# The first four modulation blocks as TensorE products with their weights resident, and the first two norms' sums and roots ahead of them, in a two-layer diffusion backbone

## What is computed

```python
def rms_norm(x):
    return x * lax.rsqrt(jnp.mean(x * x, axis=-1, keepdims=True) + EPS)
def modulate(h, shift, scale):
    return rms_norm(h) * (1 + scale) + shift
def adaln(cond, w_mod, b_mod):            # w_mod: 1024 x 6144 in each layer
    return jnp.split(jax.nn.silu(cond) @ w_mod + b_mod, 6, axis=-1)
...
sh1, sc1, g1, sh2, sc2, g2 = adaln(c, w_mod[i], b_mod[i])
csh1, csc1, ... = adaln(c_ctx, w_mod[i], b_mod[i])      # layer 0 only
out_l = mixer(modulate(h, sh1, sc1), modulate(hc, csh1, csc1), w_in, ...)
h = h + g1 * out_l
h = h + g2 * peer(modulate(h, sh2, sc2), ...)
```

## Time and profile before

| | us |
|---|---|
| median of 3 runs | 4152.5 (4149.3 to 4152.78) |
| the profiled execution, device time | 4150.12 |
| its span, first to last instruction | 4148.2 |
| TensorE busy | 3957.0 (95%) |
| VectorE busy | 2057.5 (50%) |
| ScalarE busy | 1258.6 (30%) |
| GpSimd busy | 825.1 (20%) |
| first projection matmul starts | 104.14 |

### The profile page before, as it was taken

The page is one execution under the profiler, slowest core; times in us unless marked ns, Lnnn a source line. Parts: engine busy times, 40 slices in busy tenths (PEclk is TensorE's granted clock), DMA queues, the critical chain, the costliest instruction groups (busy, mean ns, idle before and its releaser), DMA issues.

```text
span 4148.2 us, 46185 instructions
## 1 busy us (share of the span) xinstructions
PE 3957.0 (95%) x18280; PEld 3182.4 (77%) x18280; DVE 2057.5 (50%) x3962; ACT 1258.6 (30%) x1573; POOL 825.1 (20%) x364
## 2 busy tenths in 40 slices
PE   2998898999999999999999898999999999999998
PEld 2555566888888887888888577888888887888886
DVE  5655861594333433555555241891444415555555
ACT  1003443333444442111111333333444431111111
POOL 0000003444333330000000254444333330000000
PEclk9999899999999999999999899999999999999999
DMA  6561011144455555866665121344445446666663
GB/s 212 191 227 68 16 67 71 64 150 140 146 197 178 180 200 178 272 196 196 194 189 171 47 90 47 120 142 145 175 168 189 173 174 215 195 195 191 191 195 121
DMA packets 321578, 651.02 MB, mean 157 GB/s; under 512 B 18642, under 2 KB 151379, under 8 KB 300628
## 3 DMA queue, kind: packets, MB, share of 16 engines
q1 hardware_dynamic: 321364, 648.08, 47.5%
HBM read 511.69 MB, written 136.31 MB: 156 GB/s over the span
## 4 chain that ended last, share of the span: by engine, by line
PE 92%; DVE 5%; ACT 1%; issue 1%; DMA 1%; SPq 0%; DVEq 0%; ACTq 0%
PE ps L1077 34%; PE ps L1041 34%; PE ps L1053 6%; PE ps L888 5%; PE ps L963 4%; PE ps L1015 4%; PE ps L915 1%; PE ps L858 1%; PE ps L929 1%; PE ps L999 1%; DVE macc L1202 1%; PE ps L947 1%; DVE xm L1176 1%; PE ps L845 0%; DVE rinv L1172 0%
## 5 line engine op out<-in xcount | busy, mean ns | idle before, releaser
L1133 POOL TENSOR_TENSOR Ulo<-Uraw,Uhi 128x1024 fp32r<-128x1024 f32 x256 | 643.5, 2514 | 992.6 <-ACT Uhi L731 992.6
L1077 PE MATMUL ps<-Hhi,Vhi 128*128 128x512 f32 x2048 | 798.9, 390 | 20.8 <-DVE Hlo L1510 20.8
L1041 PE MATMUL ps<-xhi,Uhi 128*128 128x512 f32 x2048 | 808.8, 395 | 0.0
L1077 PE MATMUL ps<-Hlo,Vhi 128*128 128x512 f32 x2048 | 798.6, 390 | 0.0
L1077 PE MATMUL ps<-Hhi,Vlo 128*128 128x512 f32 x2048 | 798.4, 390 | 0.0
L1041 PE MATMUL ps<-xlo,Uhi 128*128 128x512 f32 x2048 | 797.5, 389 | 0.0
L1041 PE MATMUL ps<-xhi,Ulo 128*128 128x512 f32 x2048 | 797.4, 389 | 0.0
L1493 DVE TENSOR_TENSOR Vlo<-Vraw,Vhi 128x1024 fp32r<-128x1024 f32 x256 | 313.7, 1225 | 701.0 <-ACT Vhi L787 701.0
L787 ACT CAST Vhi<-Vraw 128x1024 fp32r<-128x1024 f32 x256 | 268.3, 1048 | 1123.0 <-PE ps L1077 1101.3
L1077 PEld LDWEIGHTS ps<-Hhi,Vhi 128*128 128x128 f32 x2048 | 385.6, 188 | 101.7 <-issue 21.6
L1077 PEld LDWEIGHTS ps<-Hhi,Vlo 128*128 128x128 f32 x2048 | 385.5, 188 | 80.4
(11 more groups left out here) (209 smaller groups left out, 4012.9 us busy)
## 6 DMA issues: line engine op xcount, KB each, us to landing
Uraw<-in_UT SPq DMA_DIRECT2D x128, 1024.0 KB, 5.3
Vraw<-in_V SPq DMA_DIRECT2D x256, 512.0 KB, 3.5
act_scratch<-act_st SPq DMA_DIRECT2D x256, 256.0 KB, 4.9
G_scratch<-G_st SPq DMA_DIRECT2D x32, 2048.0 KB, 8.1
act<-act_scratch SPq DMA_DIRECT2D x256, 256.0 KB, 3.5
Gin<-G_scratch SPq DMA_DIRECT2D x64, 1024.0 KB, 7.0
modw<-in_w_mod SPq DMA_DIRECT2D x48, 1024.0 KB, 5.1
ring<-in_query SPq DMA_DIRECT2D x8, 2048.0 KB, 7.9
```

Source lines behind the costliest of these rows:

```text
L1041: mm = nc.tensor.matmul(up_bank(m), w, x[:, k, :], start=(k == 0 and j == 0), stop=(k == KT - 1 and j == 2))
L1077: mm = nc.tensor.matmul(down_bank(d), w[m % 3][:, cols], x[m % 3][:, :], start=(m == 0 and j == 0), stop=(m == NT - 1 and j == 2))
L1133: nc.gpsimd.tensor_tensor(Ulo[slot][:, :, cols], Uraw[slot][:, :, cols], Uhi[(HP + m) % 3][:, :, :].bitcast(F32), ALU.subtract).then_inc(U ...
```

## The change

In words, by engine.

- **SP** loads the four first blocks whole (2 MB each) into one buffer of 64 KB per partition, `modall`, each with a semaphore of its own and with no wait, behind `ones`, `hT` and `ctxT`. The tables of the rotation go between block 0 and block 1, the first two chunks of projection weights before and after block 3, the other constants after them. The first half blocks of the later modulation now wait for 16 scaled tiles instead of 8.
- **ACT and PE** do the squares, their sums and the roots of both norms first, the latents ahead of the context now, with the squares in a buffer of their own (`sq0`).
- **PE** then forms the modulation itself (`modulation_by_rows`): for each block, for each of its 4 groups of 128 columns, 8 products over the feature tiles that add up in PSUM. 128 x 128 of `w_mod` is the stationary operand; `condS[:, k, :]`, two columns (both conditioning vectors), moves.
- **DVE** has no part in the sums of the first four blocks; `maccx` is gone. It forms EPS and reciprocals, then the modulation vectors, then scales.
- The first projection waits for its tiles one by one; `x_ready` 2*KT is asked for at the first job of chunk 1.

```diff
-        maccx = sb("maccx", 56, [P, 2, CW])
+        modall = sb("modall", 56, [P, 2 * D // CW, KT, CW])
+        rinvc = sb("rinvc", 124, [P, TC])
+        sq0 = sb("sq0", 198, [P, 2, T])
...
-        NORMS = [(ctxT, TC, xc, 0, sh1, sc1, 1), (hT, T, xm, 0, sh1, sc1, 0), (hT, T, xm, 0, sh2, sc2, 0),
+        NORMS = [(hT, T, xm, 0, sh1, sc1, 0), (ctxT, TC, xc, 0, sh1, sc1, 1), (hT, T, xm, 0, sh2, sc2, 0),
...
+            sp.dma_start(ones[:, :], a["ones"]).then_inc(consts_in, 16)
...
+            sp.dma_start(hT[:, :, :], a["xT"].rearrange("(k p) t -> p k t", p=P)).then_inc(h_in, 16)
+            sp.dma_start(ctxT[:, :, :], a["ctxT"].rearrange("(k p) t -> p k t", p=P)).then_inc(ctx_in, 16)
+            for c in range(NFIRST):
+                sp.dma_start(modall[:, c, :, :],
+                             a["w_mod"][0].rearrange("(k p) n -> p k n", p=P)[:, :, c * CW:(c + 1) * CW]
+                             ).then_inc(modall_in[c], 16)
...
+                if c >= 2:
+                    load_chunk(W_IN + c - 2)
...
-                    sp.wait_ge(x_scaled, KT)
+                elif mslot[m] == 2:
+
+                    sp.wait_ge(x_scaled, 2 * KT)
...
+            act_e.wait_ge(h_in, 16)
+            stats(0)
+            act_e.wait_ge(ctx_in, 16)
+            stats(1)
             act_e.wait_ge(mod_ready, 1)
-            norm(0)
-            norm(1)
+            shift(0)
+            shift(1)
...
+            def modulation_by_rows(i):
+
+                for j in range(4):
+                    col = (4 * i + j) * 2
+                    for k in range(KT):
+                        mm = nc.tensor.matmul(ps[:, 7, col:col + 2], modall[:, i, k, j * P:(j + 1) * P],
+                                              condS[:, k, :], start=(k == 0), stop=(k == KT - 1))
+                mm.then_inc(mod_mm, 1)
...
             norm(0)
 
-            pe.wait_ge(rinv_ready, 1)
+            pe.wait_ge(ms_ready, 1)
             norm(1)
-
-
+            for i in range(NFIRST):
+                pe.wait_ge(modall_in[i], 16)
+                modulation_by_rows(i)
...
+                if c == 1 and in_jobs[j - 1][4] == 0:
+                    pe.wait_ge(x_ready, 2 * KT)
                 for k in range(KT):
+                    if j == 0:
+                        pe.wait_ge(x_ready, k + 1)
...
+            dve.wait_ge(consts_in, 48)
+            stats(0)
+            stats(1)
+            modulation(0, 0, g1, 2)
+            dve.sem_inc(mod_ready, 1)
+            scaled(0)
+            scaled(1)
```

More of the change, by code:

```diff
@@ L270, in backbone @@
         consts_in = sem("consts_in")
-        x_in = sem("x_in")
+        h_in = sem("h_in")
+        ctx_in = sem("ctx_in")
+        tab_in = sem("tab_in")
+        modall_in = [sem(f"modall_in{c}") for c in range(2 * D // CW)]
         w_in = [sem(f"w_in{n}") for n in range(RING + 1)]
@@ L364, in backbone @@
         NH1 = 2 * NFIRST
-        mslot = [m % 2 if m < NH1 else m % 3 for m in range(2 * NCH)]
-        mbefore = [max([w for w in range(m) if mslot[w] == mslot[m]], default=None) for m in range(2 * NCH)]
-        mlanded = [16 * (1 + sum(mslot[w] == mslot[m] for w in range(m))) for m in range(2 * NCH)]
+        mslot = [m % 3 for m in range(2 * NCH)]
+        mbefore = [m - 3 if m - 3 >= NH1 else None for m in range(2 * NCH)]
+        mlanded = [16 * (1 + sum(mslot[w] == mslot[m] for w in range(NH1, m))) for m in range(2 * NCH)]
         MOD_AT = [1 + i * (len(in_jobs) - 5) // (NCH - NFIRST) for i in range(NCH - NFIRST)]
@@ L466, in load_chunk @@
                              ).then_inc(w_in[slot_of[n]], 16)
[L468 to L473, removed]
+            sp.dma_start(hT[:, :, :], a["xT"].rearrange("(k p) t -> p k t", p=P)).then_inc(h_in, 16)
[4 more added lines that the diff above has]
+                             ).then_inc(modall_in[c], 16)
+                if c == 0:
+                    for dst, name in ((cosT, "cosT"), (sinT, "sinT"), (rot, "rot"), (lamin, "lam"),
+                                      (sublg, "subln_g")):
+                        sp.dma_start(dst[tuple(slice(None) for _ in dst.shape)], a[name]).then_inc(tab_in, 16)
+                if c >= 2:
+                    load_chunk(W_IN + c - 2)
+            for dst, name in ((ident, "ident"), (iota, "iota"), (iota16, "iota16"), (iota8, "iota8"),
+                              (fing, "final_g"), (bu, "bu"), (mask, "mask"), (ones_row, "ones_row")):
+                sp.dma_start(dst[tuple(slice(None) for _ in dst.shape)], a[name]).then_inc(tab_in, 16)
             def load_mod_half(m):
                 if mbefore[m] is not None:
-                    sp.wait_ge(mod_read, mbefore[m] + 1)
-                if m >= NH1 and mslot[m] == 2 and mbefore[m] is None:
-                    sp.wait_ge(x_scaled, KT)
+                    sp.wait_ge(mod_read, mbefore[m] - NH1 + 1)
+                elif mslot[m] == 2:
+                    sp.wait_ge(x_scaled, 2 * KT)
                 layer, c, half = m // (2 * NMOD), m // 2 % NMOD, m % 2
@@ L485, in load_mod_half @@
                              ).then_inc(mod_in[mslot[m]], 16)
[L487 to L493, removed]
+            events = [(-1 if before[n] is None else chunk_used(before[n])[1], "chunk", n) for n in range(2, NIN)]
+            events += [(0 if mbefore[m] is None else MOD_AT[mbefore[m] // 2 - NFIRST] + 1, "half", m)
+                       for m in range(NH1, 2 * NCH)]
             for _, what, n in sorted(events):
@@ L624, in norm @@
                     at_least(act_e, sq_used, n * KT + k - 1)
-                    nc.scalar.activation(sq[:, k % 2, 0:width], src[:, k, :], ACT.Square).then_inc(sq_ready, 1)
+                    nc.scalar.activation(SQ[n][:, k % 2, 0:width], src[:, k, :], ACT.Square).then_inc(sq_ready, 1)
                 if while_summed is not None:
@@ L628, in norm, with shift @@
                 act_e.wait_ge(ms_ready, n + 1)
-                nc.scalar.activation(rms[:, 0:width], rms[:, 0:width], ACT.Sqrt).then_inc(rms_ready, 1)
-                if sh is None:
-                    return
+                nc.scalar.activation(RINV[n][:, 0:width], RINV[n][:, 0:width], ACT.Sqrt).then_inc(rms_ready, 1)
+            def shift(n):
+                src, width, dst, layer, sh, sc, who = NORMS[n]
                 for k in range(KT):
@@ L836, in modulation @@
             def modulation(i):
-                pe.wait_ge(macc_ready, i + 1)
+                pe.wait_ge(macc_ready, i - NFIRST + 1)
                 if i == NFIRST:
@@ L842, in modulation @@
                 for j in range(4):
[L843 to L846, removed]
+                    col = (4 * i + j) * 2
+                    mm = nc.tensor.matmul(ps[:, 7, col:col + 1], macc[:, i % 2, j * P:(j + 1) * P],
+                                          ones[:, 0:1], start=True, stop=True)
                 mm.then_inc(mod_mm, 1)
-            pe.wait_ge(x_in, 16 * 16)
-            for i in range(NFIRST):
-                modulation(i)
+            def modulation_by_rows(i):
+                for j in range(4):
+                    col = (4 * i + j) * 2
+                    for k in range(KT):
+                        mm = nc.tensor.matmul(ps[:, 7, col:col + 2], modall[:, i, k, j * P:(j + 1) * P],
+                                              condS[:, k, :], start=(k == 0), stop=(k == KT - 1))
+                mm.then_inc(mod_mm, 1)
             def norm(n):
@@ L857, in norm @@
                     pe.wait_ge(sq_ready, n * KT + k + 1)
-                    nc.tensor.matmul(ps[:, NORM_BANK[n], 0:width], ones[:, :], sq[:, k % 2, 0:width],
+                    nc.tensor.matmul(ps[:, NORM_BANK[n], 0:width], ones[:, :], SQ[n][:, k % 2, 0:width],
                                      start=(k == 0), stop=(k == KT - 1)).then_inc(sq_used, 1)
+            pe.wait_ge(consts_in, 48)
+            pe.wait_ge(cond_ready, 1)
             norm(0)
-            pe.wait_ge(rinv_ready, 1)
+            pe.wait_ge(ms_ready, 1)
             norm(1)
+            for i in range(NFIRST):
+                pe.wait_ge(modall_in[i], 16)
+                modulation_by_rows(i)
+            pe.wait_ge(tab_in, 16 * 13)
             pe.wait_ge(rinv_ready, 2)
-            pe.wait_ge(x_ready, 2 * KT)
             def rotate(rope):
@@ L1158, in modulation @@
                 step(nc.vector.scalar_tensor_tensor(
-                    out=mods[:, layer, n0:n1, 0:who], in0=sums, scalar=float(D),
+                    out=mods[:, layer, n0:n1, 0:who], in0=sums, scalar=1.0 if (layer, n0) == (0, 0) else float(D),
                     in1=bmod[:, layer, n0:n1].unsqueeze(2).to_broadcast([P, n1 - n0, who]),
@@ L1167, in norm, with stats, scaled @@
             def norm(n):
+                stats(n)
+                scaled(n)
+            def stats(n):
+                width, inv = NORMS[n][1], RINV[n]
+                dve.wait_ge(sq_used, (n + 1) * KT)
+                nc.vector.tensor_scalar(inv[:, 0:width], ps[:, NORM_BANK[n], 0:width], EPS, None, ALU.add
```

(11 more changed lines are left out.)

22 lines of the change are left out of this document (10 added, 12 removed).

## The result

| | before | after |
|---|---|---|
| median of 4 runs, us | 4152.59 (4149.3 to 4152.78) | 4127.65 (4123.64 to 4130.48) |
| ratio | | 0.9941, 95% interval 0.9924 to 0.9958 |
| the profiled execution, its span | 4150.12, 4148.2 | 4127.76, 4126.0 |
| first projection matmul | 104.14 | 79.70 |

A forecast was written before the change was run, and what follows sets the result against it. TensorE was taken to bound the kernel, idle on the chain chiefly at the start. First projection at 83.0 instead of 104.14 gives 4150.12 - 21.1 = 4129.0, plus 2.4 to the median: 4131.4 us, range 4102 to 4138.

The forecast's parts named there:

- DVE's sums, 45 us: Start of the kernel: DVE's 64 sums for the first four blocks go, 45 us from 19.13 to 64.2, all on the path.
- The norms ahead: Before the products: norms' sums and roots move ahead, first sum at 11.6 us, context's sums done at 28.6 us.
- The products' clock: TensorE's 256 product instructions run mostly at 1.2 GHz, 0.2135 us each; they take 52.4 us and end at 81.0.
- the other side: Products on TensorE: the clock stays up, 0.109 us per instruction, first projection at 58.5, total 4104.5 us; chance 0.14.
- step 2: Norms' sums and roots ahead of the products: sums begin at 11.6 us and end at 28.6 us.
- step 4: Between the last product and the first projection: 2.0 us for DVE's small steps, scaling and shifting tile 0.
- That rival: Products on TensorE keep the full clock at 0.109 us each and end at 56.5; total 4104.5 us; chance 0.14.
- From the products to the projection: Behind the products: DVE's steps 0.45 us, first tile scaled and shifted 1.55 us; first projection at 83.0 us.
- The rest at nothing: Reciprocals, context scaling, lambda and later half blocks cost nothing on the path; up to 1 us could show.
- The last step, to the median: Whole kernel: the runs' median lies 2.4 us above the profiled execution, so 4129.0 becomes 4131.4 us.
- The rival in which the products wait for each other: Products on TensorE: each instruction takes its whole 0.352 us, 90.1 us in all, first projection at 120.7, total 4169; chance 0.05.
- the head start is lost: Later blocks' transfers start too late or DVE's later sums pace the projections; time comes back, 4152 us; chance 0.05.

The follow-up runs named there:

- norms-first run: Kernel before with only the norms' squares, sums and roots moved ahead and the first projection waiting by tiles; DVE keeps its sums: 4125.11 us, ratio 0.9944.
- products-only run: Changed kernel with the norms put back in full behind the two-column products on TensorE: 4149.54 us, ratio 1.0001 against the kernel before.

## Why the prediction was right, point by point

1. *DVE's sums, 45 us.* Right as a reading, but to call it the first term overstated it. The norms-first run keeps the sums and is as fast as the changed kernel. Taken by itself the exchange of 45 us for some 50 brings nothing, and the products-only run measures just that.
2. *The norms ahead.* The first sum was forecast at 11.6 and is at 11.76, the latents' sums took 9.3 for 10.1, the gap 1.92 for 1.9, the context's sums 4.7 for 5.0; products from 27.53 for 28.6. This part, with the wait by tiles, carries the whole gain.
3. *The products' clock.* This was the step in doubt, at 0.14 for the other side. The clock fell, as the slow sums behind L845 in the earlier trace rows had suggested; their 0.2135 us held in the products-only run (54.74 us for 256). Two slips change nothing: the stretch from 64.35 on is 16 instructions, 8 products, and the limit given as 0.290 us comes to 0.287. The full clock lasted 5.2 us into the products, not the 2.5 taken from the fall at 95.3, and so they took 49.86 for 52.4. That row was of an idle engine; the fall here came while it worked. These 2.5 us and the 1.1 of step 2, less the 0.3 of step 4, are the difference between 79.70 and 83.0. That rival's price was right too: had the clock stayed up, 4104.5 was worked out, and the runs that make it stay up have 4103.3 and 4104.6 (of the half clock behind the start, which it left out, the second has some 3 us).
   The forecast's reason was that products like those of L845 don't bring the clock up. The products-only run shows it for two columns, over 54.74 us, and in the runs with 64 and 128 columns, with the same loads, it stayed up.
   The sentence of the Trainium skill in "TensorE: Matmul & The Clock Gate", Part 1, that sustained activity releases the throttle, does not hold as it stands: 54.74 us of uninterrupted TensorE work in the products-only run released nothing. The measurement decides.
4. *From the products to the projection.* 2.0 forecast, 2.3 measured.
5. *The rest at nothing.* Right for the waits that it names. DVE ends lambda at 87.25 and is asked for the first rotation at 89.56. The fifth block's first sum is 26.1 us behind the first projection and waits for no transfer. But nothing was put down for stretches at half clock further on, and the first profile lost 2.2 us of its lead there.
6. *The last step, to the median.* The 2.4 us between the profiled execution and the median held for the kernel before; the changed kernel's profile lies at its median (4127.76 and 4127.65). With the first projection at 79.70 the sum would have given 4128.1. That this is within 0.5 us of the median is luck in part: the 2.4 too much and the 2.2 lost cancel.

The rival in which the products wait for each other is out: 0.112 us for each of 256 instructions that add up eight by eight in one place. That the head start is lost is out as well, but for the 1 to 5 us that stretches at half clock took in single executions.

## What to carry to other kernels

When a change moves work to another engine and reorders the work around it, price the two apart: here the order carried all of the gain, and with two columns moving the old engine would have done as well. An instruction of these float32 products took 0.11 us at 2.4 GHz with 2, 64 and 128 moving columns, so moving more of them up to 128 was free in time and, in the runs with 64 and 128, kept TensorE at 2.4 GHz: 24 us for two changed operands. Check a stretch of such products by the duration of its weight loads (190 or 333 ns), not by TensorE's busy share, which was full in both cases. And after an idle gap has been filled, look whether the time is still there further on: here 2.0 us at the first projection were 0.3 at the first rotation.

## What the runs showed of the hardware that was not expected

- Idle columns pay: the kernel that moves each pair of columns 64 times is 24.3 us faster (4127.65 to 4103.31) than the one that moves it once, and 24.2 us faster than the one that moves it 16 times, run beside it (4127.55).
- The run with 32 columns has 4127.55 us and the one with 64 has 4104.56; no run came out between the two.
- The clock column can read 1.00 where the engine ran at 1.2 GHz, up to the first fall that it shows, which in the products-only run comes near 90 us. From 60 to 70 us it reads 1.00 there, with 48 instructions in 10 us and loads of 333 ns, the pace of 1.2 GHz. The prediction had seen the same at 64 to 68 us of the kernel before.

```profile
60.00:70.00 10.00, 10.00 (x48) 10.00 (x49) 0.00 (x0) 0.00 (x0) 0.00 (x0) 1.00 0.01 2
```
